# A convolution's input projection as block products in seven products, with the weights' rests on GpSimd

## What is computed

```python
def short_conv_mixer(h, w_in, conv_w, w_out):
    bcx = h @ w_in                                  # 512 x 1024 by 1024 x 3072
    b_gate = bcx[..., :D_MODEL]
    c_gate = bcx[..., D_MODEL:2 * D_MODEL]
    xp = bcx[..., 2 * D_MODEL:]
    u = c_gate * xp
    u_conv = causal_depthwise_conv3(u, conv_w)      # three taps along the tokens
    return (b_gate * u_conv) @ w_out
...
h = h + short_conv_mixer(rms_norm(h, conv_norm[j]), conv_w_in[j], conv_w[j], conv_w_out[j])
h = h + swiglu(rms_norm(h, ffn_norm[i]), ffn_w_gate[i], ffn_w_up[i], ffn_w_down[i])
```

## Time and profile before

| | us |
|---|---|
| median of three runs | 1075.84 (1075.51 to 1076.53) |
| the profiled execution, its device time | 1076.47 |
| its span | 1074.7 |

### The profile page before, as it was taken

The page is one execution under the profiler, slowest core; times in us unless marked ns, Lnnn a source line. Parts: engine busy times, 40 slices in busy tenths (PEclk is TensorE's granted clock), DMA queues, the critical chain, the costliest instruction groups (busy, mean ns, idle before and its releaser), DMA issues.

```text
span 1074.7 us, 17101 instructions
## 1 busy us (share of the span) xinstructions
PE 1061.0 (99%) x6496; PEld 950.1 (88%) x6496; DVE 777.6 (72%) x1081; ACT 488.8 (45%) x685; POOL 40.2 (4%) x22
## 2 busy tenths in 40 slices
PE   8999999999999999999999999999999999999997
PEld 7888888889999999888888888888999999988885
DVE  6667775999999998634447455778999999873342
ACT  6677763745544555421231212355455544651221
POOL 0232220000000000000000000000000000000000
PEclk9999999999999999999999999999999999999999
DMA  7321121232233222223322332322332233223201
GB/s 261 123 68 41 50 77 62 95 118 101 94 117 117 90 105 107 90 96 108 108 79 79 118 118 79 111 85 79 118 117 96 99 117 117 99 87 108 107 29 78
DMA packets 16959, 106.11 MB, mean 99 GB/s; under 512 B 1888, under 2 KB 2144, under 8 KB 6432
## 3 DMA queue, kind: packets, MB, share of 16 engines
q1 hardware_dynamic: 16848, 105.43, 27.5%
q0 software_dynamic: 80, 0.26, 0.1%
HBM read 103.59 MB, written 2.10 MB: 98 GB/s over the span
## 4 chain that ended last, share of the span: by engine, by line
PE 95%; DVE 1%; ACT 1%; issue 1%; DMA 1%; SPq 0%; DVEq 0%; ACTq 0%
PE bank L458 31%; PE bank L459 31%; PE bank L460 31%; PE bank L618 1%; PE bank L604 1%; ACT split L1038 1%; DMA head<-head_in 1%; DVE s_lo L1523 0%; PE bank L497 0%; DVE head L1717 0%; PE bank L606 0%; PE bank L503 0%; PE bank L511 0%; ACT a_hi L815 0%; DVE work L1516 0%
## 5 line engine op out<-in xcount | busy, mean ns | idle before, releaser
L801 ACT ACTIVATE split<-raw 128x2048 fp32r<-128x2048 f32 (+2 forms) x58 | 103.5, 1784 | 241.2 <-PE bank L460 241.1
L459 PE MATMUL bank<-x_lo,split 128*128 128x256 f32 (+1 forms) x704 | 204.0, 290 | 0.0
L458 PE MATMUL bank<-x_hi,split 128*128 128x256 f32 (+1 forms) x704 | 203.9, 290 | 0.0
L460 PE MATMUL bank<-x_hi,split 128*128 128x256 f32 (+1 forms) x704 | 203.7, 289 | 0.0
L1181 DVE TENSOR_TENSOR split<-raw,split 128x2048 fp32r<-128x2048 f32 (+2 forms) x50 | 108.6, 2171 | 101.8 <-ACT split L801 101.8
L458 PE MATMUL bank<-inner_hi,split 128*128 128x512 f32 x352 | 136.9, 389 | 0.0
L459 PE MATMUL bank<-inner_lo,split 128*128 128x512 f32 x352 | 136.9, 389 | 0.0
L460 PE MATMUL bank<-inner_hi,split 128*128 128x512 f32 x352 | 136.9, 389 | 0.0
L458 PEld LDWEIGHTS bank<-x_hi,split 128*128 128x128 f32 x704 | 132.3, 188 | 3.0 <-issue 0.5
L459 PEld LDWEIGHTS bank<-x_lo,split 128*128 128x128 f32 x704 | 132.2, 188 | 3.0 <-issue 0.5
L458 PE MATMUL bank<-x_hi,s_hi 128*128 128x256 f32 x480 | 134.1, 279 | 0.6 <-ACT work L1048 0.6
(11 more groups left out here) (200 smaller groups left out, 1912.0 us busy)
## 6 DMA issues: line engine op xcount, KB each, us to landing
raw<-weights_in SPq DMA_DIRECT2D x82, 1024.0 KB, 4.8
raw<-weights_in SPq DMA_DIRECT2D x12, 768.0 KB, 4.2
raw<-weights_in SPq DMA_DIRECT2D x6, 512.0 KB, 3.8
work<-x SPq DMA_DIRECT2D x4, 512.0 KB, 6.1
head<-head_in SPq DMA_DIRECT2D x3, 512.0 KB, 8.8
out<-head SPq DMA_DIRECT2D x3, 512.0 KB, 3.3
out<-head SPq DMA_DIRECT2D x2, 256.0 KB, 4.0
head<-head_in SPq DMA_DIRECT2D x1, 293.5 KB, 3.4
```

Source lines behind the costliest of these rows:

```text
L458: pe.matmul(o, lhs[0], rhs[0], start=start, stop=False, skip_group_check=True)
L459: pe.matmul(o, lhs[0], rhs[1], start=False, stop=False, skip_group_check=True)
L460: return pe.matmul(o, lhs[1], rhs[0], start=False, stop=stop, skip_group_check=True)
L801: act.activation(w_hi[s][:, 0:n], raw[s][:, 0:n], ACT.Copy).then_inc(hi_split[s], 1)
```

## The change

Chunks 2 to 11 of the twelve are done in the block form. Their weights are laid out in block order, their bank groups alternate (4 to 7 for even chunks, 0 to 3 for odd ones), and TensorE takes the eight forms of the activations from `A` (the four plain ones) and from two new buffers, `tail_hi` and `tail_lo`. ScalarE and VectorE fill these between the last down projection and the first block chunk: `conv_scaled`, `conv_forms`, `conv_tail_hi`, `conv_tail_rest`, for four pairs of tiles in two buffers in turn. GpSimd makes the rests of chunks 2 to 13 (10 block chunks and the first two of the output projection), L460 and L439 of the new kernel, and for each triple but the first the scaling of B and of C (L466). VectorE makes no rest of a whole chunk in this stretch any more, but the sums and their rests, and the four quarters of each block chunk; the convolution of triple m is done by `conv_mix(m)` in the first chunk of the next triple, ahead of that chunk's `top_left`, and by `conv_mix(6)` after the last chunk.

```diff
+        rstd2 = tile(work, 3)
+        mix_b, mix_y, mix_u = ([tile(mix, w + b) for b in range(2)] for w in (0, 2, 4))
...
+            def block_rest(s):
+                pool.wait_ge(hi_split[s], T.add(f"slot{s}") - 1)
+                pool.tensor_tensor(block_lo[s][:, :], raw[s][:, :], block_hi[s][:, :], ALU.subtract).then_inc(w_split[s], 1)
+            def scaled(tiles, scale):
+                pool.wait_ge(part_summed, T.add("summed"))
+                for t in tiles:
+                    pool.tensor_tensor(t, t, scale, ALU.mult).then_inc(part_scaled, 1)
+            for c in range(1, 12):
+                part = c % 3
+                if part == 1 and c > 3:
+                    scaled(mix_b, rstd[:, :])
+                if part == 2 and c > 3:
+                    scaled(mix_y, rstd2)
+                if part == 0 or c == 2:
+                    T.add("summed", int(c > 2))
+                if c < 11:
+                    block_rest((c + 1) % 2)
+            split(0)
+            split(1)
...
-            for c in range(12):
-                chunk(c % 2, [2 * (c % 3), 2 * (c % 3) + 1], A, ready=made if c == 0 else None)
-                if c == 0:
-                    stat(6, KD)
+            chunk(0, [0, 1], A, ready=made)
+            stat(6, KD)
+            chunk(1, [2, 3], A)
+            pe.wait_ge(x_split, T.add("x", K_PAIRS))
+            for c in range(2, 12):
+                winograd(c % 2, (GATE_BANK, UP_BANK)[c % 2], conv_block)
...
+            conv_scaled(0)
+            conv_scaled(1)
+            conv_tail_hi(0)
+            conv_scaled(2)
+            conv_tail_hi(1)
+            conv_scaled(3)
+            conv_tail_hi(2)
+            conv_tail_hi(3)
+            T.add("x", K_PAIRS)
+            rms(6, D)
+            blocks_hi(0)
+            sums_hi_of(0)
...
+            for c in range(2, 12):
+                g, other = c % 2, 1 - c % 2
+                if c == 2:
+                    copy(g, 1)
+                    copy(g, 5)
+                if c == 11:
+                    split(other)
+                else:
+                    blocks_hi(other)
+                if c > 2:
+                    copy(g, 1)
+                if c < 11:
+                    sums_hi_of(other)
+                if c > 2:
+                    copy(g, 5)
+                if c % 3 == 0:
+                    taps(c // 3 * 2 - 2)
+                copy(g, 6)
+                copy_last(g)
+            split(1)
+            taps(KD - 2)
...
+            def part_corner(g, dst):
+                done(g)
+                b = (GATE_BANK, UP_BANK)[g]
+                v.wait_ge(drained[b], T.add(f"b{b}"))
+                drain(b + 3, v.tensor_tensor(dst(1, 0), bank[b + 3][:, 0:HT], copies[g][0], ALU.add))
+                v.tensor_tensor(dst(1, 1), copies[g][0], copies[g][1], ALU.add).then_inc(part_summed, 1)
+                T.add("parts")
...
+            forms(0)
+            conv_forms(0)
+            conv_forms(1)
+            conv_tail_rest(0)
+            conv_forms(2)
+            conv_tail_rest(1)
+            conv_forms(3)
+            conv_tail_rest(2)
+            conv_tail_rest(3)
+            done(0)
+            inverse_rms(6)
+            do(v.tensor_tensor(rstd2, rstd[:, :], rstd[:, :], ALU.mult))
+            for b in range(2):
+                drain(b, v.tensor_tensor(mix_b[b], bank[b][:, :], rstd[:, :], ALU.mult))
+            T.add("slot0")
+            sums_rest(0)
+            forms(1)
+            done(1)
+            settle()
+            for b in range(2):
+                drain(2 + b, v.tensor_tensor(mix_y[b], bank[2 + b][:, :], rstd2, ALU.mult))
...
+            for c in range(2, 12):
...
+                if c < 11:
+                    sums_rest(1 - g)
+                if c < 10 and part == 0:
+                    forms(g)
+                if part == 0:
+                    conv_mix(m - 2)
+                top_left(g, dst)
+                if c < 10 and part != 0:
+                    forms(g)
+                top_right(g, dst)
+                part_corner(g, dst)
+                if part == 2:
+                    conv_product(m)
```

120 lines of the change are left out of this document (76 added, 44 removed).

## The result

| | before | after |
|---|---|---|
| median | 1075.67 us | 1124.79 us (1122.67 to 1128.64) |
| the profiled execution | 1076.47 | 1122.67 |
| its span | 1074.7 | 1120.6 |

The ratio is 1.0467, with a 95% interval of [1.0453, 1.0481]: 49.1 us slower. The forecast was 1122.5, 46.6 over before.

A forecast was written before the change was run, and what follows sets the result against it. TensorE was taken to bound the kernel before, VectorE and GpSimd taking turns after. The changed stretch, block saving included, gave +41.9 and the end +4.7, together +46.6 on the median: 1122.5 us, range 1086 to 1134.

The forecast's parts named there:

- wait in chunks 4, 7, 10: TensorE's wait for a ScalarE copy ahead of product 6: 8.2 us with contention in both directions, 4 without disturbance.
- a triple: Three block chunks with VectorE and GpSimd taking turns: 43.9 us, where TensorE needs 29.7 and took 32.6.
- wait for its tile 6: Output projection: GpSimd's last rest delays the last convolution, tile 6 ready at 734.2 instead of 729.5: +4.7 us.
- TensorE's saving: Ten changed chunks: block form takes 9.89 us a chunk instead of 10.88, saving 9.9 us in all.
- The opening: Between last down projection and chunk 2: activation forms stand without cover, so TensorE waits 8.8 us.
- Contention: Changed stretch: VectorE and GpSimd SBUF reads block each other both ways, a whole 4.6 us per rest; chance 0.65.
- only GpSimd gives way: Rival: VectorE runs as if alone, GpSimd's rests stretch to 6 to 9 us; +36.8, 1112.6 us; chance 0.15.
- they don't disturb each other: Rival: no contention between VectorE and GpSimd, only the opening and `top_left` count; 1088.4 us; chance 0.14.
- The convolution: Chunks 3, 6, 9: convolution ahead of `top_left` delays `copy_last` and TensorE; 13.0 us for the three, without contention.
- the clock, put at 0: Half clock after four long waits: at most 11.3 us, nothing in the sum, the 11.3 put into the range.
- the walk: Step-by-step timing of the changed stretch from row durations, with both-way contention: TensorE ends at 721.3, +41.9 us.
- The rival on the other side: Faster: activation forms hidden and `top_left` ended by 11.4 gives -9.9, 1066 us; chance 0.03.

The follow-up runs named there:

- The kernel that gained: Third six-block-chunk kernel: against the second, product 5 copied earlier in chunk 3, last scaling earlier and output projection's second rest later; 1070.59 us, ratio 0.9963.
- the same kernel with 27 fillers: Changed kernel with all of GpSimd's work, plus 27 matmuls into free bank 7 ahead of the wait before chunk 2; 1125.78 us.
- the first of the three kernels with six block chunks: Against the change: block form only in chunks 3, 4, 6, 7, 9, 10, GpSimd idle, activation forms beside chunks 0 to 2; 1075.45 us, ratio 1.0002.

## Why the prediction was right

Its steps against the trace, each counted from the end of chunk 1:

| step | forecast | measured |
|---|---|---|
| wait ahead of chunk 2 | 8.8 | 8.99 |
| start of chunk 3 | 21.7 | 21.9 |
| wait in chunks 4, 7, 10 | 8.2 | 7.9, 8.0, 8.0 |
| a triple | 43.9 | 43.8 (613.73, 657.52) |
| start of chunk 11 | 140.7 | 142.6 |
| start of the output projection | 150.9 | 153.25 |
| wait for its tile 6 | 4.7 | 3.6, after 0.7 at its start |

- **TensorE's saving.** A block chunk without a wait takes 9.80 to 9.89 in most of the kernels (10.08 over part of the one with small GpSimd instructions, at a granted clock of 1.00); this term was right and, as forecast, was not what decided.
- **The opening.** Right step for step. With GpSimd's work made small the wait is still 6.2: it is the length of the chain of forms, root and reciprocal.
- **Contention.** The step with the least evidence, both directions at the full length of a rest, holds: 26.2 of the 49.1 us are gone when GpSimd only writes. The rivals "only GpSimd gives way" and "they don't disturb each other" fall with the same rows. GpSimd's rests are 4.51 to 4.86 long, not 6 to 9, and VectorE's 1.74 becomes 4.80 to 6.17. (The terms that the first of the two lists for VectorE make 21.8 a triple and not 21.3; that moves it by 1.5 us and decides nothing.) The split of the sum came out less well than the sum: 12.6 without contention and 34.0 for it were forecast, 22.9 (1098.61) and 26.2 were measured. Without the collisions the clock's loss behind the waits lies open; with them most of it is covered. That the total is right to 2.3 us rests on this cover, which the prediction did name.
- **The convolution.** 13.0 forecast without contention, 15.0 measured as the difference of two kernels; a part of that is the aftermath of its 3.4 to 4.9 us waits. In the change as it is, moving it gives some 2.
- **The mis-sized term: the clock, put at 0.** The prediction's reason was that TensorE is not the bound there. That holds behind chunks 4 and 7: chunks 5 and 8 start late by 1.5 and 1.7 against the walk, but their product 6 waits even so, 0.82 and 0.50, for a copy that stands behind VectorE's `forms`, and from there the walk is met again. It fails where nothing else is left to wait for: behind chunk 10's wait no more `forms` come, and GpSimd's last block rest (703.82 to 708.40) is ready when TensorE would be at full speed. Its matmuls at that place start 0.21 apart where they are 0.12 at full speed:

```profile
702.92 0.42 PE L497 MATMUL bank<-tail_lo,s_hi 128*128 128x256 f32 x1
703.13 0.41 PE L498 MATMUL bank<-tail_hi,s_lo 128*128 128x256 f32 x1
```

  Products 6 and 3 take 2.73 and 2.52 there, from 702.54 over 705.27 to 707.79, where 1.41 was counted for each: +2.4, of which 0.4 lies where the walk had TensorE wait for GpSimd. The other 2.0 and the wait for `copy_last` (0.7, not foreseen; the walk had 0.3 of slack there) make the difference between the walk's 150.9 and 153.25. Stretch and end together show 48.3 (44.3 + 4.0) for the forecast 46.6: 2.4 more in the stretch and 0.7 less behind it, where the wait is smaller by 1.1. The 49.1 of the medians lies within the spread of the executions around that. Two block products at half speed was the right size; one time of the four it counted.
- **The rival on the other side.** The kernel that gained has what this rival asked for, activation forms with a cover and quarters not behind the convolution. It also leaves GpSimd out, which was not named, and gained 4 us with six chunks instead of ten. With ten chunks, the late convolution and GpSimd's reads 47 of the 49 us stayed; ten chunks with a cover and without GpSimd, or six with it, were not tried.

## What to carry to other kernels

Work moved from VectorE to GpSimd is not beside VectorE's if both read SBUF: count the sum of the two, at GpSimd's duration of twice VectorE's, and see whether TensorE needs longer than that. Where several late chains end at one engine, the worth of mending one depends on the others (15.0 or some 2 us for the same edit), so that a part of a change, done on the engines that have room, can beat the whole. Count a wait of the engine that sets the pace with its aftermath: half speed behind a long one (1.6 to 3.9 us here), slower starts behind a short one (0.55).

## What the runs showed of the hardware beyond that

- The hold is not only for two operands. VectorE's cast of one 512-column tile takes 0.42 alone and 4.60 behind a GpSimd subtraction, a `tensor_scalar` 4.59; and a GpSimd copy, with one input, stretches a VectorE instruction from 1.76 to 3.31. Beside a GpSimd memset of 1.8 us the same instruction stays at 1.76.
- GpSimd's subtraction of 2048 columns takes 4.49 alone, VectorE's 2.28 (27.38 in the same run). The Trainium skill (GPSIMD Engine Reference, section "Elementwise — side-by-side cycle accounting") has 4497 and 2293 ns for an addition of this size; these rows agree.
- How long the clock stays down is not the same for the same wait. Behind 6.19 us it was back at 1.00 by 578 in the kernel with small GpSimd instructions (chunk 2 took 1.6 more than its matmuls and its wait) and only after 584 in the one with the convolution late (3.9 more). Nor does it fall at the same point of the wait: in the first, whose wait begins at 568.58, it is at 0.53 from 571 to 572; in the second, whose wait begins at 570.07, it is at 1.00 until 574.
- The granted clock fell in or behind every wait of 6 to 10 us and every one of 3.4 to 5.6 us in the block chunks, and behind ones of 2.84 and 2.97 with fillers ahead of them. Shorter waits, and the one for tile 6, went either way. The 3.62 us for tile 6 left it at 1.00 in the changed kernel (728 to 738); in the same kernel with 27 fillers, with the same 3.62, it was at 0.50 from 734 to 738. The changed kernel's three waits of 2.1 left it at 1.00; two of three such (2.10 and 2.14) in the kernel with all of GpSimd's work and the late convolution did not. Two waits of 1.97 at nearly the same place differ: in the first of the three kernels with six block chunks the clock stood at 0.79 over 584 to 592, in the second at 1.00. What decides between them was not tried; it may be why these kernels' executions spread over 4 to 7 us (the first over 1072.9 to 1079.6) and those of before over some 3.
- The parts of the program that no kernel changed differed from one execution to the next: in the kernel before and those with ten block chunks the end of chunk 1 lay between 568.0 and 570.5, and from the output projection's start to the last instruction it was 395.3 to 397.2 in kernels with the same waits there.
